# The opening of a two-layer diffusion step in four pieces of two chunks, with six column groups accumulated at once

## What is computed

```python
mod = silu(cond) @ w_mod[l] + b_mod[l]              # cond: c_ctx for the prompt, c for the sample
sh1, sc1, g1, sh2, sc2, g2 = split(mod, 6)          # 1024 columns each
h = rms_norm(x, g_pre_mix) * (1.0 + sc1) + sh1
proj = h @ w_in                                     # lru_x, lru_gate, q, kv, k_rope, merge gates
xc = centred_conv(proj[lru_x], conv_w, conv_b)      # the RG-LRU branch, 1024 channels
```

## Time and profile before

| | us |
|---|---|
| median of 3 runs | 1260.92 |
| lowest and highest | 1258.25, 1262.77 |
| the profiled execution | 1262.09 |
| its span | 1260.2 |
| TensorE busy | 1233.3 (98%) |
| VectorE busy | 847.9 (67%) |
| ScalarE busy | 639.8 (51%) |

### The profile page before, as it was taken

How to read it: one execution, slowest core, us unless ns; L and a number is a source line. 1 busy time by engine, 2 the same in 40 slices (tenths; PEclk the granted TensorE clock), 3 DMA queues, 4 the chain that set the end, 5 groups by cost and what they waited for, 6 DMA issues and landing times.

```text
span 1260.2 us, 19229 instructions
## 1 busy us (share of the span) xinstructions
PE 1233.3 (98%) x7345; PEld 1145.0 (91%) x7345; DVE 847.9 (67%) x1325; ACT 639.8 (51%) x1129; POOL 19.6 (2%) x41
## 2 busy tenths in 40 slices
PE   6999999999999999999999999999999999999998
PEld 4899999988879999998879999998897999999886
DVE  2697584774868888868858895857666748433433
ACT  5477863764464333332254989557546433333322
POOL 0000000200000000000000000020000000000000
PEclk9999999999999999999999999999999999999999
DMA  9635555333347776758814333442233446344451
GB/s 334 220 115 183 176 177 199 106 119 125 105 133 235 246 225 199 234 176 277 285 49 145 103 116 117 134 139 84 72 97 134 138 141 227 120 132 134 159 167 50
DMA packets 131102, 199.32 MB, mean 158 GB/s; under 512 B 10330, under 2 KB 70980, under 8 KB 131012
## 3 DMA queue, kind: packets, MB, share of 16 engines
q1 hardware_dynamic: 131012, 198.11, 48.9%
HBM read 196.16 MB, written 1.92 MB: 157 GB/s over the span
## 4 chain that ended last, share of the span: by engine, by line
PE 95%; ACT 1%; DVE 1%; DMA 1%; issue 1%; SPq 1%; DVEq 0%; ACTq 0%
PE bank L762 21%; PE bank L769 21%; PE bank L770 20%; PE bank L892 6%; PE bank L893 6%; PE bank L894 6%; PE bank L1192 2%; PE bank L1216 1%; PE bank L1201 1%; PE bank L799 1%; ACT sq L1330 1%; DMA first_mod<-in_w_mod 1%; PE bank L1036 1%; PE bank L1038 1%; PE bank L1037 1%
## 5 line engine op out<-in xcount | busy, mean ns | idle before, releaser
L769 PE MATMUL bank<-act_low,weight_high 128*128 128x384 f32 x1440 | 486.6, 338 | 0.0
L770 PE MATMUL bank<-act_high,weight_low 128*128 128x384 f32 x1440 | 483.4, 336 | 0.0
L1692 DVE TENSOR_TENSOR weight_low<-raw,weight_high 128x1024 fp32r<-128x1024 f32 (+5 forms) x282 | 320.0, 1151 | 147.7 <-ACT weight_high L1322 146.7
L1322 ACT ACTIVATE weight_high<-raw 128x1024 fp32r<-128x1024 f32 (+5 forms) x282 | 273.7, 996 | 236.5 <-DMA raw<-in_w_ffn_in 77.3
L762 PE MATMUL bank<-act_high,weight_high 128*128 128x384 f32 x1440 | 316.1, 340 | 1.8 <-ACT act_high L1407 1.2
L769 PEld LDWEIGHTS bank<-act_low,weight_high 128*128 128x128 f32 x1440 | 272.0, 189 | 3.3 <-issue 3.2
L770 PEld LDWEIGHTS bank<-act_high,weight_low 128*128 128x128 f32 x1440 | 271.9, 189 | 0.0
L762 PEld LDWEIGHTS bank<-act_high,weight_high 128*128 128x128 f32 x1440 | 253.3, 189 | 10.5 <-issue 5.2
L892 PE MATMUL bank<-weight_high,hid_high 128*128 128x512 f32 x264 | 103.2, 391 | 0.0
L894 PE MATMUL bank<-weight_high,hid_low 128*128 128x512 f32 x264 | 102.8, 389 | 0.0
L893 PE MATMUL bank<-weight_low,hid_high 128*128 128x512 f32 x264 | 102.8, 389 | 0.0
(11 more groups left out here) (265 smaller groups left out, 1443.5 us busy)
## 6 DMA issues: line engine op xcount, KB each, us to landing
raw<-in_w_ffn_in SPq DMA_DIRECT2D x176, 256.0 KB, 4.2
mod_weight<-in_w_mod SPq DMA_DIRECT2D x80, 512.0 KB, 4.6
raw<-in_w_in SPq DMA_DIRECT2D x72, 512.0 KB, 3.7
raw<-in_w_ffn_out SPq DMA_DIRECT2D x44, 512.0 KB, 4.5
first_mod<-in_w_mod SPq DMA_DIRECT2D x4, 2048.0 KB, 13.7
raw<-in_w_o_lru SPq DMA_DIRECT2D x16, 512.0 KB, 3.7
raw<-in_w_out SPq DMA_DIRECT2D x16, 512.0 KB, 3.7
raw<-in_w_o_mla SPq DMA_DIRECT2D x8, 512.0 KB, 4.3
```

Of the source, the lines that this page charges most:

```text
L769: nc.tensor.matmul(o, view[0][:, kk, cols], low[:, k, :], start=False, stop=False)
L770: ins = nc.tensor.matmul(o, view[1][:, kk, cols], high[:, k, :], start=False, stop=k == total - 1)
L1322: nc.scalar.activation(high, w, ACT.Copy).then_inc(*AC.step())
L1692: nc.vector.tensor_tensor(low, w, high.bitcast(F), ALU.subtract).then_inc(*VE.step())
```

## The change

- The modulation is cut into four **pieces** q of two chunks (256 columns of the shift, 256 of the scale), each a product, a copy, a fold and an addition of its own; eight DMAs of 1 MB in place of four of 2 MB.
- The first eight weight loads hold other parts of the same 1024 columns (`FIRST_LOADS`: first chunk, chunks, first column, columns): four **wide** loads (two chunks, the 512 columns of `lx0`), two **pair** loads (four chunks, the first 256 columns of `lx1`), two of the **rest** (four chunks, the last 256 columns of `lx1`). Wide loads are read in runs of 512 columns as before, pair and rest loads in runs of 256.
- `first_piece(q)` accumulates six column groups for its two chunks (four of `lx0`, two of `lx1`), 36 matmuls, with the products and folds of piece q+1 hooked in before its matmuls number 6, 12, 20 and 25. After the fourth piece `first_rest` does the last two groups of `lx1` over all eight chunks, 48 matmuls.
- VectorE scales x into `ybuf` (`scaled`, six instructions), and TensorE transposes it (`turned`); ScalarE's three diagonal matrices go. ScalarE moves all eight chunks out of PSUM, 6 and 7 into `sq`.
- On VectorE the low part of a wide load comes between a chunk's `t` and its low part, and the steps of the eight chunks no longer overlap by one.

```diff
-NEXT = range(4)
-FIRST = ((0, 2), (1, 3))
+FIRST_LOADS = ((0, 2, 0, 512), (0, 4, 512, 256), (2, 2, 0, 512), (4, 2, 0, 512), (4, 4, 512, 256), (6, 2, 0, 512),
+               (0, 4, 768, 256), (4, 4, 768, 256))
+FIRST_WIDE = (0, 2, 3, 5)
+FIRST_PAIR = (1, 4)
+FIRST_REST = (6, 7)
...
+        def moved(c):
+            return qkv[:, c, :] if c < 6 else sq[c - 6]
...
+            def first_mods(kind, q):
+                c0 = D * kind + 256 * q
+                sp.dma_start(first_mod[:, 2 * q + kind, :, :], A["w_mod"][0:1, :, c0:c0 + 256].rearrange("a (k p) n -> p (a k) n", p=P)
+                             ).then_inc(start_mod[kind][q], 16)
...
+                    first_mods(0, 0)
                     vector_rows(0)
-                    first_mods(FIRST[0][1:])
+                    first_mods(1, 0)
                 for n, load in enumerate(LOADS):
-                    if n == 2 and l == 0:
-                        first_mods(FIRST[1])
-                    if n == 4 and l == 0:
+                    if n in FIRST_WIDE[1:] and l == 0:
+                        first_mods(0, FIRST_WIDE.index(n))
+                        first_mods(1, FIRST_WIDE.index(n))
+                    if n == FIRST_REST[0] and l == 0:
                         constants_in()
...
+                    parts = load.parts
+                    if l == 0 and n < len(FIRST_LOADS):
+                        k0, kc, c0, cols = FIRST_LOADS[n]
+                        parts = [("rows", "w_in", k0, kc, OFF_LX + c0, cols, 0)]
+                    for part in parts:
                         if part[0] == "rows":
                             _, name, k0, kc, c0, cols, o = part
-                            dst = slot[:, 0:load.kc * load.cols].rearrange("p (k n) -> p k n", n=load.cols)
+                            width = load.kc * load.cols // kc
+                            dst = slot[:, 0:load.kc * load.cols].rearrange("p (k n) -> p k n", n=width)
                             src = A[name][layer:layer + 1, k0 * P:(k0 + kc) * P, c0:c0 + cols]
                             sp.dma_start(dst[:, :, o:o + cols], src.rearrange("a (k p) n -> p (a k) n", p=P)
                                          ).then_inc(*full.step(by=16))
...
+                def first_product(kind, q):
+                    pe.wait_ge(start_mod[kind][q], 16)
+                    if q == 1:
+                        pe.wait_ge(*at(AC, "moved", 6 + kind))
+                    elif q > 1:
+                        pe.wait_ge(*at(VE, "added", kind, q - 1))
+                    o = ps[2 + kind if q == 0 else 6 + kind]
...
+                def first_piece(q):
+                    count = [0]
+                    hooks = {6: lambda: first_product(0, q + 1), 12: lambda: first_fold(0, q + 1),
+                             20: lambda: first_product(1, q + 1), 25: lambda: first_fold(1, q + 1)} if q < 3 else {}
+                    def product(o, weights, acts, c, last=False):
+                        if count[0] in hooks:
+                            hooks[count[0]]()
+                        count[0] += 1
+                        return nc.tensor.matmul(o[:, 0:T], weights, acts, start=last is None and c == 0, stop=bool(last))
+                    for n, job, banks, base in ((FIRST_WIDE[q], "lx0", range(4), 0), (FIRST_PAIR[q // 2], "lx1", range(2), 0)):
+                        s = n % SPL
+                        k0, kc, _, cols = FIRST_LOADS[n]
+                        high, low = ([w[:, 0:kc * cols].rearrange("p (k n) -> p k n", n=cols)] for w in (wh[s], wl[s]))
+                        pe.wait_ge(*at(AC, "high", n))
+                        for c in (2 * q, 2 * q + 1):
+                            pe.wait_ge(*at(AC, "hh", "mix", c))
+                            for g in banks:
+                                product(bank(job, g), high[0][:, c - k0, P * g:P * g + P], hh[:, c, :], c, None)
+                            pe.wait_ge(*at(VE, "low", n))
+                            pe.wait_ge(*at(VE, "h", "mix", c))
+                            for g in banks:
+                                product(bank(job, g), high[0][:, c - k0, P * g:P * g + P], hl[:, c, :], c)
+                                ins = product(bank(job, g), low[0][:, c - k0, P * g:P * g + P], hh[:, c, :], c, c == C - 1)
+                                if c == C - 1:
...
+                        for kk in range(4):
+                            c = 4 * half + kk
+                            for g in range(2):
+                                o = bank("lx1", 2 + g)[:, 0:T]
+                                cols = slice(P * g, P * g + P)
+                                nc.tensor.matmul(o, high[:, kk, cols], hh[:, c, :], start=c == 0, stop=False)
+                                nc.tensor.matmul(o, high[:, kk, cols], hl[:, c, :], start=False, stop=False)
+                                ins = nc.tensor.matmul(o, low[:, kk, cols], hh[:, c, :], start=False, stop=c == C - 1)
+                                if c == C - 1:
...
                     late_turned(4)
-                    first_product(0, 1)
                     late_turned(5)
-                    first_fold(0, 1)
+                    first_product(1, 0)
                     late_turned(6)
                     late_turned(7)
-                    split_job("lx0", hh, hl, ready=(VE, "h", "mix"), ready_high=(AC, "hh", "mix"), between=opening_between)
+                    first_fold(1, 0)
+                    for q in range(4):
+                        first_piece(q)
+                    first_rest()
...
+                    def move(chunks):
+                        for c in chunks:
+                            ac.wait_ge(*at(PE, "turned", "mix", c))
+                            nc.scalar.activation(moved(c), turn_bank("fo", c)[:, 0:T], ACT.Copy).then_inc(*AC.step("moved", c))
+                    def first_high(c):
+                        ac.wait_ge(*at(VE, "hfull", "mix", c))
+                        nc.scalar.activation(hh[:, c, :], t[c % 2][:, :], ACT.Copy).then_inc(*AC.step("hh", "mix", c))
+                    move(range(6))
+                    for q in range(4):
+                        highs("lx0", 0, ahead=FIRST_WIDE[q])
+                        first_high(2 * q)
+                        if q == 0:
+                            move((6, 7))
+                        first_high(2 * q + 1)
+                        if q % 2 == 0:
+                            highs("lx0", 0, ahead=FIRST_PAIR[q // 2])
...
+                if l == 0:
+                    for a in range(3):
+                        scaled("mix", 0, a)
+                    first_copy(0, 0)
+                    ve.wait_ge(*at(PE, "par"))
+                    nc.vector.tensor_copy(par[:, :], ps[0][:, 0:NA + NB]).then_inc(*VE.step())
+                    own()
+                    first_add(0, 0)
+                    first_copy(1, 0)
+                    for q in range(4):
+                        first_add(1, q)
+                        gain(scale1, 1, "g_pre_mix", ("scale1", q), slice(2 * q, 2 * q + 2))
                         own()
...
+                        first_shift(2 * q)
+                        lows("lx0", 0, ahead=FIRST_WIDE[q])
+                        first_low(2 * q)
+                        first_shift(2 * q + 1)
+                        first_low(2 * q + 1)
+                        if q < 3:
+                            first_copy(0, q + 1)
+                        if q % 2 == 0:
+                            lows("lx0", 0, ahead=FIRST_PAIR[q // 2])
+                        if q < 3:
+                            first_add(0, q + 1)
+                            first_copy(1, q + 1)
                 own()
 
                 nc.vector.tensor_scalar(lam[3][:, :], par_cols("lru_lambda"), -1.0, None, ALU.mult).then_inc(*VE.step())

```

More of the change, by code:

```diff
@@ L977, in first_fold @@
-                def first_fold(half, i):
-                    r = FIRST[half][i]
-                    pe.wait_ge(start_fold, 16)
-                    pe.wait_ge(*at(VE, "first", r))
-                    for g in range(4):
-                        ins = nc.tensor.matmul(ps[(1, 4)[half]][:, 8 * i + 2 * g:8 * i + 2 * g + 2],
-                                               tok_flat[:, 512 * r + P * g:512 * r + P * g + P], fold[:, :],
-                                               start=i == 0 and g == 0, stop=True, skip_group_check=True)
-                    ins.then_inc(*PE.step("first_fold", r))
```

135 lines of the change are left out of this document (58 added, 77 removed).

## The result

The changed kernel takes **1263.79 us** (median; 1261.72 to 1264.71) against 1260.90 of the kernel before (1258.19 to 1262.77), ten runs each: ratio 1.0025, interval 1.0016 to 1.0033. That is inside the range and inside the 0.3% of "no change", but the forecast said 1.6 us earlier and it came 2.9 later. The interval excludes a gain. That the range held it is luck: its upper end stood for one or two late boundaries between the pieces, and none came.

A forecast was written before the change was run, and what follows sets the result against it. TensorE, busy 98%, was taken as the bound, its start set by DMA bytes. Start 20.4 plus body 45.3 gave 65.7; a 1.65 clock drop made 67.35, 1.6 earlier: 1260.92 - 1.6 = 1259.3 us, range 1255 to 1264.

The forecast's parts named there:

- one or two late boundaries between the pieces: Range's upper end, 1264: VectorE's additions late between pieces, a single such boundary giving +1.2 us.
- The transfers: Opening DMA in 1 KB runs: 0.87 per share, 3.1 us per MB; shift lands at 11.9, scale at 16.5.
- The wait of 0.6 that I gave the second shift: First piece: TensorE asks for the second shift at 21.9, it lands at 22.5.
- The sum without clock: Branch start to `qk` without a clock drop: body 45.3 us, ending at 65.7, 3.2 earlier than 68.93.
- The start, step by step: Opening: scale lands at 16.5, product 1.1, copy 0.42, fold 0.5, tail 1.77; branch starts at 20.4, 6.4 earlier.
- all under the wait for the scale: Opening: turning and squaring of x end before the scale lands at 16.5; 1 us if that cover were gone.
- The sentences that TensorE stayed at its upper level before 42: Grounds for the no-clock-drop rival (28 in 100; 3.2 earlier, 1257.7): upper level held through gaps of 1.46 and 0.37.
- The clock: Around the new start, 16.5 to 21.9: one drop to half clock costing 1.65 us, bounds 0 and 3.3.
- The slack falls from 5.4 to 0.6, but stays: nothing: Behind the body: VectorE's low part for `qk` comes 15.1 into the fourth piece, needed at 15.7; no cost.
- The waits inside a piece: Body: TensorE waits 0.45 us a piece for VectorE's low parts, 1.8 in all; bounds 0 and 1.2 each.
- VectorE late at every piece: Rival, 8 in 100: late additions at three boundaries, 1.18 wait plus 1.65 clock each; +6.9, 1267.8 us.
- Nothing arrives: Rival, 10 in 100: VectorE's thin slack behind the body, or slower 1 KB runs, eat the lead; about 1260.5 us.

The follow-up runs named there:

- run 5: Changed kernel plus 27 fill matmuls in TensorE's idle stretches before the branch and the small constants of VectorE moved into the second piece; 1258.69 us, ratio 0.9981.
- run 1: Changed kernel plus 27 fill matmuls (128x128, results overwritten) on TensorE before the branch; 1260.63 us, ratio 1.0002.
- run 10: Changed kernel plus only the 16 later fill matmuls, behind the first turned tiles, ahead of the second product and ahead of the branch; 1260.49 us, ratio 1.0003.
- run 3: Kernel before with only the turning of x changed: VectorE scales, TensorE transposes; 1262.57 us, ratio 1.0019.
- run 4: Changed kernel with the small constants of VectorE, and ScalarE's steps between, moved from behind the fourth piece into the second; 1261.69 us, ratio 1.0009.
- run 7: Changed kernel with only the wide loads' low parts moved earlier on VectorE, ahead of the copy of the next product; 1262.70 us, ratio 1.0016.
- run 6: Changed kernel plus 27 fill matmuls, small constants in the second piece, and wide loads' low parts earlier on VectorE; 1258.95 us, ratio 0.9987.
- run 2: Changed kernel with x turned and scaled by the fp32 matmul with a diagonal, as in the kernel before; 1262.37 us, ratio 1.0016.
- run 9: Changed kernel plus only the 11 early fill matmuls, ahead of the first turned tiles; 1262.34 us, ratio 1.0014.
- run 8: Control: kernel before plus 11 fill matmuls ahead of its first turned tiles; 1260.58 us, ratio 0.9998.

## Why the prediction was wrong

Step by step, changed kernel (profiled) against forecast, and beside it run 5, where the clock is held and the constants are out of the way:

| | forecast | changed | run 5 |
|---|---|---|---|
| branch starts | 20.4 | 23.38 | 20.92 |
| from there to `qk` | 46.95 | 46.3 | 44.9 |
| of it a drop of the clock | 1.65 | 1.5 | 0 |
| `qk` starts | 67.35 | 69.70 | 65.79 |
| wait behind it | 0 | 1.3 | 0 |
| gates start | | 74.62 | 69.25 |

The 1.5 is the changed kernel's 46.3 less the 44.8 of run 1.

- **The transfers were right.** The trace gives 8.4 us from issue (3.35) to landing for the first shift and 6.1 for the first scale (issue 10.08): about 11.8 and 16.2, where I had 11.9 and 16.5. In the stretch from 30 to 40 us of the changed kernel, with runs of 1 KB and 2 KB mixed, DMA moved 354 GB/s at a share of 1.09, against 387 at 1.05: 0.88 per share, where I took 0.87. The figure worked out from the Trainium skill ("DMA: Bandwidth & Descriptors", "Why small descriptors are slow (HBM only)"), 0.96, does not agree with that row. The wait of 0.6 that I gave the second shift did not come: in run 5 TensorE asks at 22.49 and finds it there. Its body is 0.4 shorter than the sum, about as much.

```profile
30.00:40.00 10.00, 9.89 (x78) 7.86 (x77) 4.75 (x12) 2.00 (x3) 0.00 (x0) 1.00 1.09 354
```

- **The sum without clock was right**: `qk` at 65.7 by the forecast, 65.79 in run 5.
- **The step that failed is "The start, step by step": every term behind 16.5 at full rate (product 1.1, fold 0.5) and the turning "all under the wait for the scale".** The scale was there at 16.2, but TensorE, at half rate, was still turning and began the product at 18.00; it took 1.94. That is 2.5 us of the start by run 1 (23.38 against 20.89), and the sum had nothing for it. I had read the granted clock of the page and not the lengths: the eight records of 2.04 at 8.96, against 1.16 at 16.71, say that the kernel before starts at half rate too, and its first product of 2.57 against 1.92 for the second says that the clock came up only within it. The sentences that TensorE stayed at its upper level before 42 and that the gaps before 27 were at full clock are wrong for all that stands ahead of this rise.
- **"The clock" itself came as forecast**: one drop, priced 1.65, between 18 and 26. It measured 1.5 and stood from 24.3 to 27.7. Both losses together are 4.0 in the profiled pair, above my bound of 3.3, and 3.2 in the medians.
- **What brings the first rise late is shown in part.** Fill takes both losses away in the traces of runs 1 and 10, so they hang on what TensorE does in these stretches. That the cheaper turning is at fault, less work ahead of the product, is argued: run 3 is slower in the median and its first product takes 3.64, but the traces of runs 4 and 7 have the cheap turning and an early rise.
- **The second failure is "The slack falls from 5.4 to 0.6, but stays: nothing".** For the first low part of `qk` that was right: it ended at 69.45 for a need at 70.39. But I followed VectorE to that low part only. The copies for the gates come behind three low parts of `qk` and wait for nothing else; run 4 takes the constants out and the wait is gone, run 5 against run 1 prices it at 1.9 us in the median and 1.4 in the trace (70.62 to 69.25). The prediction's own count, carried on, would have shown it: the copies end 5.1 behind the low part (69.45 to 74.52), so 20.2 into the fourth piece, and the gates stand 3.5 behind the start of `qk`, so 18.5; an estimate of 1.7 us of wait, and 1.29 came.
- **The waits inside a piece were right**: 1.8 for four, and the list says 1.6. Run 6 recovers 0.9 of it in the body and loses 0.7 at the start.
- **The rivals.** "VectorE late at every piece" did not happen: no boundary waited over 0.4, and behind 27.7 the clock stayed up in spite of them. The rule of "TensorE: Matmul & The Clock Gate" in the Trainium skill, "A second HAM failure mode: psum-queue depth-cycling", gave those boundaries the clock's swing; the rows show a drop at the start instead, behind a wait of 1.8 us and not of 0.4, and in run 2 no drop behind the same wait. "Nothing arrives" had one half of its reason right, VectorE behind the body, with too small a price.
- **Of its own signs of being wrong** two came: the first matmul after 22 and `qk` later than 68.9. The third, over 0.6 of idling at a boundary, did not.

Of the measured +2.9, the profiled pair gives 2.2: the start 3.4 earlier (26.77 to 23.38), the way to `qk` 4.2 longer (46.3 against 42.2), the way from there to the gates 1.45 longer, 1.29 of it the wait. The rest, 0.7, lies between profiled executions and medians: the kernel before was profiled 1.2 above its median, the changed one 0.5.

What stays open: run 5 has its gates 3.15 us earlier than the kernel before, but a span only 1.7 shorter and a median 2.0 lower, so 1.45 us of the trace and 1.2 of the median go somewhere behind 70 us. The traces say that this part differs by itself: from the gates to the end run 5 takes 1189.25, and run 6, whose edit differs from run 5 only ahead of the gates, 1187.05. Half-rate stretches come and go there: from 365 to 375 us the mean granted clock is 0.83 in the traces of the kernel before and of run 5, 1.00 in those of the changed kernel and run 6. I did not separate the two.

## What to carry to other kernels

Where the opening of a kernel waits for data, TensorE's work between the waits also sets at which clock it meets the data. Before making that work cheaper, read the lengths of equal instructions early and late: a factor of nearly two, as here with 2.04 and 1.16, says that the clock is not up yet, and an opening shortened on paper may run at half rate. Fill matmuls placed in the waits between the first tiles and the branch gave 3 us here (run 10); placed earlier they gave half of that at most, not clear of the noise (run 9), and in the kernel before nothing (run 8). When work is compressed on one engine, follow the other engines' backlog past the first consumer, to the last that needs a buffer or a bank from it.

## What was unexpected of the hardware

- The granted clock in the profile says 1.00 for a stretch that ran at half rate. In the changed kernel the window from 8 to 20 us gives (length; busy and count of PE, PEld, DVE, ACT, POOL; clock, DMA share, GB/s):

```profile
8.00:20.00 12.00, 9.49 (x57) 5.92 (x58) 3.59 (x9) 8.06 (x23) 0.00 (x0) 1.00 1.07 329
```

It holds both products of 1.94, which take 1.07 in run 1, while the drop behind 24 us is in the column as 0.50. So 1.00 there doesn't prove full rate in the opening; the length of a known instruction is the surer sign.
- The same instructions meet the clock at another level from one execution to the next: the second product took 1.94 in the changed kernel, 1.07 in runs 4 and 7, whose TensorE program is the same. Executions of one kernel differ by 2 to 7 us, as much as the effects studied here (run 1: 1259.6 to 1261.6; run 3: 1259.3 to 1266.1). That the clock of the opening makes this spread is not shown, since each kernel has one trace.
- A wait doesn't settle the clock by its length: 1.80 us ahead of the branch stands in the traces of the changed kernel and of runs 2, 4 and 9, and a drop follows in three of them, not in run 2. In the kernel before, the drop of 43 stood behind 1.18.
